# Norm and pooling work in half rows, placed by lateness, and down products added two banks at a time, in a streaming encoder step on one Trainium2 core

## The chip, the cores and the metric

The kernel runs on one core of one Trainium2 chip. The metric is device time in microseconds of one execution, on that core. The engines are TensorE (PE in the profile), VectorE (DVE), ScalarE (ACT), GpSimd (POOL) and SyncE (SP, which here only issues DMAs).

## The reference

Two layers over 1056 tokens (1024 of a prompt and 32 of a running stream), width 1024, float32. Cut to what matters:

```python
for i in range(2):
    y = short_conv_mixer(x) if i == 0 else pool_mixer(x)      # pooling: trailing means over 2, 4, 8, 16 frames, by four groups of channels
    h = layer_norm(ALPHA * x + y, ln1_g[i], ln1_b[i])          # called ("mix", i, group) below
    r = relu(h @ mlp_w1[i])                                    # 1024 -> 4096, the "up" products
    f = (r * r) @ mlp_w2[i]                                    # 4096 -> 1024, the "down" products
    e = (p[i] @ ple_w[i]) * sigmoid(h @ ple_gate_w[i])         # the "ple" and "gate" products
    x = layer_norm(ALPHA * h + f + e, ln2_g[i], ln2_b[i])      # called ("mlp", i, group)
```

In the pooling mixer, `d = means - x` and `y = (d @ w_grp) * scale`, with one 256x256 matrix for each of the four channel groups (the "grp" products).

## The kernel before, in words

Activations lie transposed: 128 features on the partitions, tokens along the free axis. The 1056 tokens are three groups (n = 0, 1, 2) of TG = 352, and a row of 1024 features is 8 blocks (KD) of 128 features. `acc` holds the residual of all three groups, 8x352 columns each. Every product is made in three matmuls on split operands (`triple`: high by high, high by low, low by high), so each weight and each activation has a high part, cast by ScalarE, and a low part, subtracted by VectorE. A weight unit of 128x1024 is loaded by SP into one of four raw buffers, cast (L727) and subtracted (L549); this is called a refill here.

The program is one list of steps, `plan`, and each engine walks through the whole list in order and does its part of each step. The kinds that matter:

- an up step: 24 matmuls on TensorE into one bank; then ScalarE makes relu (L841), square (L843) and the high part `r_hi` (L847); then VectorE subtracts the low part `r_lo` (L1042). Up steps come in pairs; they are called the first and the last up step here.
- a down step: 24 matmuls, 6 for each of four blocks, into four PSUM banks in turn; VectorE adds each bank to `acc` (L1046) and so frees it. Down steps come in pairs as well: the first for blocks 0 to 3, the second for blocks 4 to 7, in the same four banks. So the second cannot begin before VectorE has added block 0 of the first: the line is `pe.wait_ge(b_free, step.b + (i - 3))`.
- a gate step (24 matmuls) and a ple step (6 matmuls) for the gated embedding.

The usual order is up, up, down, down. The down steps use `r` of the pair of up steps before the last one, so TensorE doesn't wait for fresh `r` values.

After its own work of a step, an engine does first the step's refills and then the step's `side` list: the pieces of layer norm and pooling that the planner has hung on that step. VectorE and ScalarE do them in this order, and nothing of the next step overtakes them. The pieces of a norm on VectorE are sum (L935 to L937), mean (L966, subtracts the mean), vsum (the same tree on the squares), var (L971), rstd (L975 reciprocal, L977 to L979), norm (L983, multiplies) and lo (L986, the low part of the result); on ScalarE square, affine (L786) and hi (L803). TensorE makes the means with matmuls by ones, at L654 and L658. The pieces of pooling, for each of four windows, are fill (ScalarE copies to a window buffer), the running sums on GpSimd (L1126), centre (VectorE, L999, L1005, L1009), grp (12 matmuls on TensorE for two output blocks, which wait for centre's result) and gadd (VectorE, L1018).

Where each piece is hung is decided by `beside`: it goes through rows of (gap, cost, pieces), moves on by gap steps, and on until three steps in a row have `cost` microseconds left of what `room` gives them. LEAD says how many chunks of the MLP group 0 does alone, and how many groups 0 and 1 do together, before group 2 joins, in each layer.

Of the kernel before, what the change touches and what calls it, by code (L numbers as in the profile page):

```python
# [12 lines left out]
P = 128  # L13
# [23 lines left out]
LEAD = (5, 3), (9, 5)  # L37
# [6 lines left out]
MM_US, ADD_US, GATE_US, R_LO_US, SPLIT_US = 0.159, 0.52, 0.57, 0.61, 1.23  # L44
# [107 lines left out]
def make_plan():  # L152
# [99 lines left out]
    def room(step):  # L252

        own = len(step.refill) * SPLIT_US
        if step.kind == "down":
            return 24 * MM_US - own - 4 * ADD_US
        if step.kind == "up":
            return 24 * MM_US - own - R_LO_US
        if step.kind == "gate":
            return 30 * MM_US - own - 2 * GATE_US  # L260
        return 24 * MM_US - own - 2 * ADD_US

    def norm(i, done):

        n = NORMS.index(i)
        rows = [(0, 3.2, [("sum", n, done)]), (2, 3.1, [("mean", n)]), (1, 0, [("square", n)]), (1, 3.2, [("vsum", n)]), (2, 0.6, [("var", n)]),
                (1, 4.0, [("rstd", n)]), (1, 3.1, [("norm", n)]), (1, 0, [("affine", n, 0)]), (1, 0, [("affine", n, 1)])]
        if i[0] == "mix":
            rows += [(1, 0, [("hi", n)]), (1, 3.1, [("lo", n)])]
        return rows  # L270

    def pooling(n):
        rows = [(1, 0, [("fill", 4 * n)]), (1, 0, [("fill", 4 * n + 1)])]
        for q in range(len(WINDOWS)):
            rows.append((1, 3.0, [("centre", 4 * n + q)]))
            if q + 2 < len(WINDOWS):
                rows.append((0, 0, [("fill", 4 * n + q + 2)]))
            if q:
                rows.append((1, 1.1, [("grp", 8 * n + 2 * q - 2 + j, 4 + (q - 1) // 2) for j in range(2)]
                             + [("gadd", 8 * n + 2 * q - 2 + j) for j in range(2)]))  # L280
        rows.append((2, 1.1, [("grp", 8 * n + 6 + j, 5) for j in range(2)] + [("gadd", 8 * n + 6 + j) for j in range(2)]))
        return rows

    def beside(first, *chains, grp_from=0):


        steps = [s for s in plan[first:] if s.kind not in ("ple", "refill")]
        at = 0
        for row in (row for chain in chains for row in chain):
            gap, cost, parts = row  # L290
            at += gap
            while parts[0][0] == "grp" and plan.index(steps[at]) <= grp_from:
                at += 1
            while cost and sum(left[id(s)] for s in steps[at:at + 3]) < cost:
                at += 1
            steps[at].side += parts
            for s in steps[at:at + 3]:
                spent = min(cost, max(left[id(s)], 0))
                left[id(s)] -= spent
                cost -= spent  # L300
        return plan.index(steps[at])
# [37 lines left out]
    left = {}  # L339
# [4 lines left out]
    for step in plan:  # L344
        left[id(step)] = room(step)

# [36 lines left out]
def bass_streaming_trunk(nc, x_t, w_stream, p_t, vectors, conv_hist, pool_hist, y_t, conv_new, pool_new):  # L383
# [6 lines left out]
    with ExitStack() as ctx:  # L390
# [167 lines left out]
        def _(sp):  # L558
# [38 lines left out]
            for n in range(NG - 1):  # L597
                for h in range(2):

                    sp.wait_ge(affine, (len(NORMS) - NG + n) * 2 + h + 1)  # L600
# [11 lines left out]
        def _(pe):  # L612
# [25 lines left out]
            def side(what, i, *rest):  # L638
# [16 lines left out]
                elif what == "var":  # L655
                    pe.wait_ge(var_sum, i + 1)
                    pe.wait_ge(centred, i + 1)
# [16 lines left out]
            def do(step):  # L674
# [6 lines left out]
                elif step.kind == "gate":  # L681
                    if step.m == 0:
                        pe.wait_ge(h_ready, step.layer * NG + step.n + 1)
# [34 lines left out]
        def _(act):  # L718
# [43 lines left out]
            def side(what, i, *rest):  # L762
                if what == "finish":
# [4 lines left out]
                    side("var", i)  # L768
# [4 lines left out]
                elif what == "square":  # L773
                    act.wait_ge(centred, i + 1)
                    act.activation(grp(squares, NORMS[i][2]), grp(acc, NORMS[i][2]), ACT.Square).then_inc(squared, 1)
                elif what == "var":
# [4 lines left out]
                elif what == "affine":  # L781
                    kind, layer, n, at = norm_of(i)
                    h, = rest
                    act.wait_ge(normed, i + 1)
                    for k in range(4 * h, 4 * h + 4):
                        last = act.activation(blk(acc, n, k), blk(acc, n, k), ACT.Identity, bias=vcol(at + KD + k), scale=vcol(at + k))  # L786
                    last.then_inc(affine, 1)
                    if (kind, layer, h) == ("mlp", 0, 1):
                        act.wait_ge(affine, 2 * i + 2)
# [7 lines left out]
                elif what == "hi":  # L797
                    kind, layer, n, _ = norm_of(i)
                    act.wait_ge(affine, 2 * i + 2)
# [3 lines left out]
                    act.copy(grp(hh, n), grp(acc, n)).then_inc(ln_hi, 1)  # L803
                elif what == "fill":
# [3 lines left out]
                    act.wait_ge(affine, 2 * NORMS.index(("mlp", 0, n)) + 2)  # L808
# [64 lines left out]
        def _(dve):  # L873
# [59 lines left out]
            def tree(src, tmp, out, done):  # L933
                h = GCOLS // 2
                then(dve.tensor_tensor(tmp[:, 0:h], src[:, 0:h], src[:, h:2 * h], ALU.add))  # L935
                then(dve.tensor_tensor(tmp[:, 0:h // 2], tmp[:, 0:h // 2], tmp[:, h // 2:h], ALU.add))
                dve.tensor_tensor(out, tmp[:, 0:TG], tmp[:, TG:2 * TG], ALU.add).then_inc(done, 1)  # L937

            def over_blocks(ap):
                return ap.rearrange("p (a t) -> p a t", a=1).to_broadcast([P, KD, TG])  # L940

            def side(what, i, *rest):
                n = NORMS[i][2] if i < len(NORMS) else None
                if what == "finish":
# [4 lines left out]
                    side("rstd", i)  # L949
# [3 lines left out]
                elif what == "sum":  # L953
                    name, value = rest[0]
                    dve.wait_ge(sems[name], value)

                    wait(dve, mean_full, i)
                    tree(grp(acc, n), grp(squares, n), s_mean[:], mean_sum)
                elif what == "vsum":
                    dve.wait_ge(squared, i + 1)  # L960

                    wait(dve, rstd_done, i)
# [243 lines left out]
```

## Time and profile before

| | us |
|---|---|
| median of 3 runs | 2201.65 (2198.06 to 2203.07) |
| the profiled execution, its own time | 2200.9 |
| its span from first to last instruction | 2199.1 |
| TensorE matmuls busy | 2130.7 (97% of the span) |
| VectorE busy | 1255.0 (57%) |
| ScalarE busy | 807.3 (37%) |
| GpSimd busy | 70.3 (3%) |
| mean granted TensorE clock | 0.990 |

The share of a busy engine counts the time in which at least one of its instructions runs. Matmuls overlap (each record lasts about 0.32 us, and one begins every 0.16 us), so the time in which TensorE has no record is a little less than what a wait costs. The span leaves 1.8 us of the execution's own time outside.

### The profile page before, as it was taken

The numbers are of one execution on the slowest core, as the hardware profiler recorded it, in microseconds if no ns is written. First come the engines' busy times: TensorE is split into PE (matmuls) and PEld (weight loads), VectorE is DVE, ScalarE is ACT, GpSimd is POOL, SyncE is SP. The second block draws the span as 40 slices with busy tenths as digits, with TensorE's granted clock in tenths as the row PEclk, the third lists the DMA queues.
The fourth block names the chain that finished last, engine by engine and source line by source line (L and its number), as shares of the span: only waits on it lengthen the run. The fifth ranks groups of instructions, "written<-read, shape, count | busy, mean of one in ns | idle before, by whom it ended". The sixth has DMA issues, their size and how long they took to land. (4 is left out here: it accounts for less than half of the span.)

```text
span 2199.1 us, 31589 instructions
## 1 busy us (share of the span) xinstructions
PE 2130.7 (97%) x13166; PEld 2113.8 (96%) x13166; DVE 1255.0 (57%) x1823; ACT 807.3 (37%) x1233; POOL 70.3 (3%) x61
## 2 busy tenths in 40 slices
PE   8999999999999999999999999998989999999996
PEld 8999999999999999999999999998989999999996
DVE  4233367786454444445676777876755355444576
ACT  3122123654333222323444455455333224233343
POOL 0000000000000000000110030002000000000000
PEclk9999999999999999999999999999999999999998
DMA  4011141343132111111212434442213112122232
GB/s 168 29 57 39 56 134 65 113 134 125 55 106 77 39 57 40 46 51 39 68 68 70 129 115 150 136 134 70 77 55 96 58 49 66 53 75 77 77 116 99
DMA packets 51455, 179.67 MB, mean 82 GB/s; under 512 B 7936, under 2 KB 8064, under 8 KB 51328
## 3 DMA queue, kind: packets, MB, share of 16 engines
q1 hardware_dynamic: 49248, 177.72, 24.4%
q8 instruction: 95, 1.56, 0.3%
q10 hardware_dynamic: 2080, 0.12, 0.1%
q14 instruction: 32, 0.26, 0.0%
HBM read 173.36 MB, written 4.46 MB: 81 GB/s over the span
## 5 line engine op out<-in xcount | busy, mean ns | idle before, releaser
L616 PE MATMUL ps<-h_hi,w_split 128*128 128x352 f32 x2160 | 700.0, 324 | 4.8 <-DVE h_lo L921 2.1
L618 PE MATMUL ps<-h_hi,w_split 128*128 128x352 f32 x2160 | 692.8, 321 | 0.0
L617 PE MATMUL ps<-h_lo,w_split 128*128 128x352 f32 x2160 | 692.2, 320 | 0.0
L616 PE MATMUL ps<-r_hi,w_split 128*128 128x352 f32 x1632 | 536.5, 329 | 37.5 <-DVE acc L1046 37.5
L618 PE MATMUL ps<-r_hi,w_split 128*128 128x352 f32 x1632 | 528.3, 324 | 0.0
L617 PE MATMUL ps<-r_lo,w_split 128*128 128x352 f32 x1632 | 527.8, 323 | 0.0
L1046 DVE TENSOR_TENSOR acc<-acc,ps 128x352 f32<-128x352 f32 x768 | 376.4, 519 | 145.1 <-PE ps L618 143.9
L549 DVE TENSOR_TENSOR w_split<-w_raw,w_split 128x1024 fp32r<-128x1024 f32 x294 | 357.0, 1232 | 136.4 <-ACT w_split L727 135.7
L727 ACT CAST w_split<-w_raw 128x1024 fp32r<-128x1024 f32 x294 | 301.6, 1046 | 322.1 <-PE ps L618 316.5
L616 PEld LDWEIGHTS ps<-h_hi,w_split 128*128 128x128 f32 x2160 | 405.0, 187 | 7.6 <-issue 3.7
L617 PEld LDWEIGHTS ps<-h_lo,w_split 128*128 128x128 f32 x2160 | 406.4, 188 | 1.1
L618 PEld LDWEIGHTS ps<-h_hi,w_split 128*128 128x128 f32 x2160 | 404.9, 187 | 0.0
L616 PEld LDWEIGHTS ps<-r_hi,w_split 128*128 128x128 f32 x1632 | 310.0, 190 | 45.1 <-issue 34.5
L1042 DVE TENSOR_TENSOR r_lo<-t,r_hi 128x352 fp32r<-128x352 f32 x192 | 101.8, 530 | 434.3 <-ACT r_hi L847 434.3
L617 PEld LDWEIGHTS ps<-r_lo,w_split 128*128 128x128 f32 x1632 | 311.2, 191 | 1.2
L618 PEld LDWEIGHTS ps<-r_hi,w_split 128*128 128x128 f32 x1632 | 309.8, 190 | 0.0
L841 ACT ACTIVATE t<-ps 128x352 f32<-128x352 f32 x192 | 89.1, 464 | 570.5 <-PE ps L618 562.4
L616 PE MATMUL ps<-x_hi,w_split 128*128 128x352 f32 x576 | 186.4, 324 | 9.2 <-DVE w_split L549 9.2
L618 PE MATMUL ps<-x_hi,w_split 128*128 128x352 f32 x576 | 186.6, 324 | 0.0
L617 PE MATMUL ps<-x_lo,w_split 128*128 128x352 f32 x576 | 185.9, 323 | 0.0
L616 PEld LDWEIGHTS ps<-x_hi,w_split 128*128 128x128 f32 x576 | 108.7, 189 | 9.2 <-issue 9.2
L618 PEld LDWEIGHTS ps<-x_hi,w_split 128*128 128x128 f32 x576 | 109.9, 191 | 0.0
(80 smaller groups left out, 1118.2 us busy)
## 6 DMA issues: line engine op xcount, KB each, us to landing
w_raw<-w_stream SPq DMA_DIRECT2D x318, 512.0 KB, 3.5
x_raw<-x_t SPq DMA_DIRECT2D x6, 704.0 KB, 8.4
y_t<-acc SPq DMA_DIRECT2D x4, 704.0 KB, 4.1
w_raw<-p_t SPq DMA_DIRECT2D x6, 352.0 KB, 2.9
y_t<-acc SPq DMA_DIRECT2D x4, 352.0 KB, 2.4
pool_new<-acc ACTq DMA_DIRECT2D x2, 60.0 KB, 7.2
vec<-vectors SPq DMA_DIRECT2D x1, 78.0 KB, 7.2
pool_history<-pool_hist SPq DMA_DIRECT2D x1, 60.0 KB, 6.7
```

The source lines that it names most:

```text
L549: ins = eng.tensor_tensor(ws[:, slot, 1, :], raw[:, u.q, :], f32(ws[:, slot, 0, :]), ALU.subtract)
L616: pe.matmul(out, wh, mov_h, start=first, stop=False)
L617: pe.matmul(out, wh, mov_l, start=False, stop=False)
L618: return pe.matmul(out, wl, mov_h, start=False, stop=last)
L727: act.copy(ws[:, slot, 0, :], raw[:, u.q, :]).then_inc(w_hi, 1)
L841: act.activation(t, ps[:, step.bank, 0:TG], ACT.Relu).then_inc(a_free, 1)
L1042: dve.tensor_tensor(rpart(rl, *r), tt[:, step.bank, :], f32(rpart(rh, *r)), ALU.subtract).then_inc(r_ready, 1)
L1046: dve.tensor_tensor(blk(acc, step.n, m), blk(acc, step.n, m), ps[:, B_BANK + (step.bank + i) % 4, 0:TG], ALU.add).then_inc(b_free, 1)
```

## The change

Norm and centre pieces are cut: sum, centre (which "mean" did before), square, vsum, rstd, norm, hi and lo have two parts each, and affine four. Most of these are two instructions of 128x1408 where one of 128x2816 stood; sum, vsum and rstd have the same instructions in two parts. The piece of pooling on VectorE is called `centre_window` and has two parts, the second of which is the subtraction of L1009. The planner's rows carry a cost on VectorE and one on ScalarE, and the rule that places them is new: a piece goes on the first step at which neither engine would then be more than LATE_US behind. The rows of the grp products of group 0 come one after the other with their windows, those of groups 1 and 2 after all four windows. GpSimd's part is as before. In layer 1 group 0 does 8 chunks alone where it did 9. VectorE adds two PSUM banks at a time in all down steps but the last two.

```diff
-LEAD = (5, 3), (9, 5)
+LEAD = (5, 3), (8, 5)
-MM_US, ADD_US, GATE_US, R_LO_US, SPLIT_US = 0.159, 0.52, 0.57, 0.61, 1.23
+MM_US = 0.159
+DVE_US = {"split": 1.23, "down": 2 * 0.89, "up": 0.61, "gate": 2 * 0.57, "out": 2 * 0.53}
+ACT_US = {"split": 1.05, "down": 0, "up": 1.45, "gate": 0.5, "out": 0}
+LATE_US = 2.4
...
+    def own(step, table):
+        return table.get(step.kind, 0) + len(step.refill) * table["split"]
...
-        rows = [(0, 3.2, [("sum", n, done)]), (2, 3.1, [("mean", n)]), (1, 0, [("square", n)]), (1, 3.2, [("vsum", n)]), (2, 0.6, [("var", n)]),
-                (1, 4.0, [("rstd", n)]), (1, 3.1, [("norm", n)]), (1, 0, [("affine", n, 0)]), (1, 0, [("affine", n, 1)])]
+        rows = [(0, 1.7, 0, [("sum", n, 0, done)]), (0, 1.5, 0, [("sum", n, 1, done)]),
+                (2, 1.6, 0, [("mean", n), ("centre", n, 0)]), (0, 1.6, 0, [("centre", n, 1)]),
+                (1, 0, 1.3, [("square", n, 0)]), (0, 0, 1.3, [("square", n, 1)]),
+                (1, 1.7, 0, [("vsum", n, 0)]), (0, 1.5, 0, [("vsum", n, 1)]), (2, 0.6, 0, [("var", n)]), (1, 0, 0.5, [("root", n)]),
+                (1, 2.4, 0, [("rstd", n, 0)]), (0, 1.6, 0, [("rstd", n, 1)]),
+                (0, 1.6, 0, [("norm", n, 0)]), (0, 1.6, 0, [("norm", n, 1)])]
+        rows += [(q == 0, 0, 1.35, [("affine", n, q)]) for q in range(4)]
...
+            rows += [(1, 1.6, 0, [("centre_window", 4 * n + q, 0)]), (0, 1.0, 0, [("centre_window", 4 * n + q, 1)])]
+            products.append((1, 1.1, 0.6 * 2, [("grp", 8 * n + 2 * q + j, 4 + q // 2) for j in range(2)]
+                             + [("gadd", 8 * n + 2 * q + j) for j in range(2)]))
+            if n == 0:
+                rows.append(products.pop())
...
+        def late(table, which, cost):
+            total = 0
+            for i, step in enumerate(steps[:at + 1]):
+                took = (30 if step.kind == "gate" else 24) * MM_US
+                total = max(0, total - took) + own(step, table) + taken[which].get(id(step), 0)
+            return max(0, total + cost - took)
...
-            while cost and sum(left[id(s)] for s in steps[at:at + 3]) < cost:
+            while ((parts[0][0] == "grp" and plan.index(steps[at]) <= grp_from)
+                   or (dve_us and late(DVE_US, "dve", dve_us) > LATE_US) or (act_us and late(ACT_US, "act", act_us) > LATE_US)):
                 at += 1
...
+                elif step.kind == "down" and not step.final:
+                    for i in range(0, len(step.blocks), 2):
+                        k, bank = step.blocks[i], B_BANK + (step.bank + i) % 4
+                        dve.wait_ge(b_full, step.b + (i + 2))
+                        two = grp3(acc, step.n)[:, k:k + 2, :]
+                        dve.tensor_tensor(two, two, ps[:, bank:bank + 2, 0:TG], ALU.add).then_inc(b_free, 2)
```

The first place in VectorE's order is the norm ("mix", 1, 1), in layer 0's last chunks. Before, from the down step that carries its var to the next up steps:

```order
L1042 TENSOR_TENSOR r_lo<-t,r_hi 128x352
L971 TENSOR_SCALAR var<-ps 128x352
L1046 TENSOR_TENSOR acc<-acc,ps 128x352 x4
L549 TENSOR_TENSOR w_split<-w_raw,w_split 128x1024
L1046 TENSOR_TENSOR acc<-acc,ps 128x352 x4
L549 TENSOR_TENSOR w_split<-w_raw,w_split 128x1024 x2
L975 RECIPROCAL std<-std 128x352
L977 SCALAR_TENSOR_TENSOR rstd<-std 128x352
L978 TENSOR_TENSOR rstd<-rstd,var 128x352
L979 SCALAR_TENSOR_TENSOR rstd<-rstd,std 128x352
L1042 TENSOR_TENSOR r_lo<-t,r_hi 128x352
```

And of the change, around the same reciprocal (L998), where L1071 is the `r_lo` of the last up step and L1077 the adds of the first down step:

```order
L553 TENSOR_TENSOR w_split<-w_raw,w_split 128x1024
L1071 TENSOR_TENSOR r_lo<-t,r_hi 128x352
L998 RECIPROCAL std<-std 128x352
L1001 SCALAR_TENSOR_TENSOR rstd<-std 128x352
L1002 TENSOR_TENSOR rstd<-rstd,var 128x352
L1003 SCALAR_TENSOR_TENSOR rstd<-rstd,std 128x352
L1008 TENSOR_TENSOR acc<-acc,rstd 128x1408
L1077 TENSOR_TENSOR acc<-acc,ps 128x704 x2
```

The reciprocal and its three followers stood behind the second down step; now they and half of the multiplication stand between the last up step's `r_lo` and the first down step's adds.

The second place is VectorE in the pooling of group 0. Before, the piece of window 0 and what stands around it:

```order
L1042 TENSOR_TENSOR r_lo<-t,r_hi 128x352 x2
L1046 TENSOR_TENSOR acc<-acc,ps 128x352 x8
L549 TENSOR_TENSOR w_split<-w_raw,w_split 128x1024 x2
L996 TENSOR_TENSOR win_54<-win_54,vec 128x2x15
L999 SCALAR_TENSOR_TENSOR win_54<-win_54,acc 128x2x352
L1005 CAST h_hi<-win_54 128x704
L1009 TENSOR_TENSOR h_lo<-win_54,h_hi 128x704
L1042 TENSOR_TENSOR r_lo<-t,r_hi 128x352
```

And of the change:

```order
L1071 TENSOR_TENSOR r_lo<-t,r_hi 128x352 x2
L1030 TENSOR_TENSOR win_54<-win_54,vec 128x2x15
L1033 SCALAR_TENSOR_TENSOR win_54<-win_54,acc 128x2x352
L1039 CAST h_hi<-win_54 128x704
L1018 TENSOR_TENSOR h_lo<-win_54,h_hi 128x704
L1077 TENSOR_TENSOR acc<-acc,ps 128x704 x2
L1047 SCALAR_TENSOR_TENSOR acc<-acc,y_scaled_t 128x352 x2
```

The window stood behind two down steps and their refills, and its products came three steps later; now it stands behind the last up step's `r_lo`, and the grp products that need it (their gadd is L1047) come behind TensorE's very next step.

The third place is the start of the norm ("mix", 1, 1), where the ple weights are loaded. Before, the refills of four units (L549 x4) and the whole sum stood behind a second down step:

```order
L549 TENSOR_TENSOR w_split<-w_raw,w_split 128x1024 x4
L935 TENSOR_TENSOR ln_squares<-acc 128x1408
L936 TENSOR_TENSOR ln_squares<-ln_squares 128x704
L937 TENSOR_TENSOR sum_mean<-ln_squares 128x352
L1042 TENSOR_TENSOR r_lo<-t,r_hi 128x352
```

And of the change:

```order
L1071 TENSOR_TENSOR r_lo<-t,r_hi 128x352
L553 TENSOR_TENSOR w_split<-w_raw,w_split 128x1024 x2
L943 TENSOR_TENSOR ln_squares<-acc 128x1408
L1077 TENSOR_TENSOR acc<-acc,ps 128x704 x2
L553 TENSOR_TENSOR w_split<-w_raw,w_split 128x1024
```

Two of the refills and the first part of the sum now stand between a last up step's `r_lo` and the first down step's adds.

## Rows read from the trace of the kernel before

**Rows 1.** The page: its head and the busy time of PE and DVE.

```profile
span 2199.1 us, 31589 instructions
PE 2130.7 (97%) x13166; PEld 2113.8 (96%) x13166; DVE 1255.0 (57%) x1823; ACT 807.3 (37%) x1233; POOL 70.3 (3%) x61
```

**Rows 2.** Waits of PE, whole span: us in total, times, longest.

```profile
PE ps L616 <- DVE acc L1046: 37.5, 19, 5.5
...
PE ps L616 <- DVE acc L1025: 2.1, 2, 1.5
```

**Rows 3.** The same by stretch: 270:520, 1000:1200, 1500:1650, 1650:2150.

```profile
PE ps L616 <- DVE acc L1046: 2.0, 2, 1.7
...
PE ps L616 <- DVE acc L1046: 10.4, 6, 2.5
...
PE ps L616 <- DVE acc L1046: 20.4, 6, 5.5
...
PE ps L616 <- DVE acc L1046: 3.1, 2, 1.9
```

**Rows 4.** Timeline of DVE at one wait: start us, us, instruction, [idle before].

```profile
1184.78 0.53 DVE L1042 TENSOR_TENSOR r_lo<-t,r_hi 128x352 fp32r<-128x352 f32 x1 [3.33 <-ACT r_hi L847]
1185.22 3.08 DVE L986 TENSOR_TENSOR h_lo<-acc,h_hi 128x2816 fp32r<-128x2816 f32 x1
1188.22 2.42 DVE L1046 TENSOR_TENSOR acc<-acc,ps 128x352 f32<-128x352 f32 x5
```

**Rows 5.** Timeline of PE there: a pair of down steps begins, stops, restarts.

```profile
1183.02 0.32 PE L616 MATMUL ps<-r_hi,w_split 128*128 128x352 f32 x1
...
1186.70 0.32 PE L618 MATMUL ps<-r_hi,w_split 128*128 128x352 f32 x1
1188.88 0.40 PE L616 MATMUL ps<-r_hi,w_split 128*128 128x352 f32 x1 [1.86 <-DVE acc L1046]
```

**Rows 6.** Timeline of DVE where two refills follow a last up step.

```profile
1577.32 0.53 DVE L1042 TENSOR_TENSOR r_lo<-t,r_hi 128x352 fp32r<-128x352 f32 x1 [1.10 <-ACT r_hi L847]
1578.27 2.36 DVE L549 TENSOR_TENSOR w_split<-w_raw,w_split 128x1024 fp32r<-128x1024 f32 x2 [0.43 <-ACT w_split L727]
1580.55 2.41 DVE L1046 TENSOR_TENSOR acc<-acc,ps 128x352 f32<-128x352 f32 x5
```

**Rows 7.** Groups of DVE: busy us, mean ns of one, idle before.

```profile
L966 DVE TENSOR_TENSOR acc<-acc,ps 128x2816 f32<-128x2816 f32 x11 | 33.9, 3081 | 0.0
...
L975 DVE RECIPROCAL std<-std 128x352 f32<-128x352 f32 x12 | 28.2, 2347 | 0.6 <-ACT std L780 0.6
...
L936 DVE TENSOR_TENSOR ln_squares<-ln_squares 128x704 f32<-128x704 f32 x22 | 19.6, 892 | 0.8
...
L935 DVE TENSOR_TENSOR ln_squares<-acc 128x1408 f32<-128x1408 f32 x11 | 17.8, 1622 | 0.2
...
L977 DVE SCALAR_TENSOR_TENSOR rstd<-std 128x352 f32<-128x352 f32 x12 | 6.3, 525 | 0.4
```

**Rows 8.** Timeline of DVE: one piece of a window, GpSimd idle, and adds behind it.

```profile
1096.71 0.89 DVE L999 SCALAR_TENSOR_TENSOR win<-win,acc 128x704 f32<-128x704 f32 x1
...
1098.20 0.89 DVE L1009 TENSOR_TENSOR h_lo<-win,h_hi 128x704 fp32r<-128x704 f32 x1
1099.01 1.81 DVE L1046 TENSOR_TENSOR acc<-acc,ps 128x352 f32<-128x352 f32 x4
```

**Rows 9.** Timeline of DVE: window and gadd while GpSimd runs.

```profile
1529.33 3.46 DVE L999 SCALAR_TENSOR_TENSOR win<-win,acc 128x640 f32<-128x640 f32 x2
...
1537.57 3.37 DVE L1018 SCALAR_TENSOR_TENSOR acc<-acc,y_scaled_t 128x352 f32<-128x352 f32 x2
```

**Rows 10.** Windows: busy us of PE, PEld, DVE, ACT, POOL, then PEclk, DMA.

```profile
1190.00:1195.00 5.00, 5.00 (x23) 5.00 (x22) 2.02 (x5) 0.09 (x1) 0.00 (x0) 0.66 0.01 3
```

**Rows 11.** Timeline of ACT ahead of the longest wait.

```profile
1510.67 2.39 ACT L786 ACTIVATE acc<-acc,vec 128x352 f32<-128x352 f32 x4
...
1515.60 0.48 ACT L847 CAST r_hi<-t 128x352 fp32r<-128x352 f32 x1
```

More of the change, by code:

```diff
@@ new lines, in pooling @@
+            if n == 0:
+                rows.append(products.pop())
+            if q + 2 < len(WINDOWS):
+                rows += [(n > 0, 0, 1.0, [("fill", 4 * n + q + 2)])]
+        return rows + products
+    def beside(first, *chains, grp_from=0):
+        steps = [s for s in plan if s.kind not in ("ple", "refill")]
+        at = next(i for i, s in enumerate(steps) if plan.index(s) >= first)
+        def late(table, which, cost):
[4 more added lines that the diff above has]
+            return max(0, total + cost - took)
+        for gap, dve_us, act_us, parts in (row for chain in chains for row in chain):
@@ L291, in beside @@
             at += gap
-            while parts[0][0] == "grp" and plan.index(steps[at]) <= grp_from:
-                at += 1
-            while cost and sum(left[id(s)] for s in steps[at:at + 3]) < cost:
+            while ((parts[0][0] == "grp" and plan.index(steps[at]) <= grp_from)
+                   or (dve_us and late(DVE_US, "dve", dve_us) > LATE_US) or (act_us and late(ACT_US, "act", act_us) > LATE_US)):
                 at += 1
             steps[at].side += parts
[L297 to L300, printed above, removed]
+            for which, cost in (("dve", dve_us), ("act", act_us)):
+                taken[which][id(steps[at])] = taken[which].get(id(steps[at]), 0) + cost
@@ L682, in do @@
                     if step.m == 0:
-                        pe.wait_ge(h_ready, step.layer * NG + step.n + 1)
+                        pe.wait_ge(h_ready, 2 * (step.layer * NG + step.n + 1))
                     if step.a < 2:
@@ L773, in side @@
                 elif what == "square":
-                    act.wait_ge(centred, i + 1)
-                    act.activation(grp(squares, NORMS[i][2]), grp(acc, NORMS[i][2]), ACT.Square).then_inc(squared, 1)
-                elif what == "var":
+                    n, h = NORMS[i][2], rest[0]
+                    act.wait_ge(centred, 2 * i + h + 1)
+                    act.activation(half(squares, n, h), half(acc, n, h), ACT.Square).then_inc(squared, 1)
+                elif what == "root":
                     act.wait_ge(var_copied, i + 1)
@@ L798, in side @@
                     kind, layer, n, _ = norm_of(i)
-                    act.wait_ge(affine, 2 * i + 2)
+                    h, = rest
+                    act.wait_ge(affine, 4 * i + 2 * h + 2)
                     if layer == 0:
                         act.wait_ge(out_full, (8, 20, 24)[n])
-                    act.copy(grp(hh, n), grp(acc, n)).then_inc(ln_hi, 1)
+                    act.copy(half(hh, n, h), half(acc, n, h)).then_inc(ln_hi, 1)
                 elif what == "fill":
@@ L972, in side @@
                 elif what == "rstd":
-                    dve.wait_ge(std_done, i + 1)
-                    wait(dve, normed, i)
-                    then(dve.reciprocal(std[:], std[:]))
+                    part, = rest
+                    if part == 0:
+                        dve.wait_ge(std_done, i + 1)
+                        wait(dve, normed, 2 * i)
+                        steps[0] += 1
+                        dve.reciprocal(std[:], std[:]).then_inc(ln_step, 1)
+                        return
+                    dve.wait_ge(ln_step, steps[0])
                     then(dve.scalar_tensor_tensor(out=rstd[:], in0=std[:], scalar=-0.5, in1=std[:], op0=ALU.mult, op1=ALU.mult))
```

112 lines of the change are left out of this document (54 added, 58 removed).

## The prediction

> **What bounds the kernel now.** I read the page first: TensorE has a matmul in flight for 97% of the span, VectorE is busy for 57%, ScalarE for 37% [rows 1]. So the number of matmuls sets the time (the change adds and takes away none), and what can move is the time in which TensorE stands still. Next the waits of TensorE over the span: 37.5 us in 19 waits go to VectorE's adds of down products, and 2.1 to those of the out products [rows 2]. By stretch they lie where norms and pooling run beside the MLP: 10.4 us around 1100, 20.4 around 1575, 3.1 in layer 1, 2.0 in the head [rows 3]; all other waits for the adds are worth 1.6. Last the timeline of one wait, on both engines, for its anatomy.
>
> **The rule of one wait.** A first down step begins on TensorE at 1183.02 [rows 5]. The last up step's `r_lo` starts 1.76 us later, at 1184.78, and the next instruction of VectorE at 1185.22, so 2.20 us after the up step's end; before that the engine was idle, waiting for ScalarE [rows 4]. There stands lo, 3.00 us from its start to that of the first add at 1188.22 [rows 4]. TensorE restarts at 1188.88, 0.66 us after that start; its last matmul began at 1186.70, so it was due at 1186.86, 3.84 us after it began [rows 5]. With S the work on VectorE between the last up step's `r_lo` and the first add, the loss is 2.20 + S + 0.66 - 3.84 = S - 0.98, here 2.02 (the profile calls 1.86 of it idle). Work behind the first down step's adds, behind the second down step or on the first up step costs nothing: VectorE is idle for 3.3 us ahead of this `r_lo` [rows 4], and that idle time is the cover. The place of a piece decides, not its length alone.
>
> **The add over two banks.** No row has one. A lower bound is the 704-column subtraction, whose successor starts 0.81 us later (1098.20 to 1099.01), against 0.43 us a piece for single adds (four in 1.81, the last lasting 0.52) [rows 8]. An upper bound is two singles without overlap, 1.04. I take 0.81, same shape and engine. VectorE saves 2 x 0.43 - 0.81 = 0.05 us a pair, so nothing that counts, and TensorE gets block 0 back 0.38 us later: the loss becomes S - 0.60. With S = 0 the slack of 0.60 hides it, at the upper bound too (0.37 left), so the 480 us in which no norm runs stay as they are. If the add is at its upper bound, the thirty or so waits below grow by 0.23 us each, 7 us in all.
>
> The Trainium skill speaks for this edit (VectorE: DVE Perf Modes, the section on the errata with its cycle table): a PSUM-source instruction costs 120 cycles beside its columns at 0.96 GHz, and one should minimise their number. By that, an estimate, a down step's adds fall from 1.97 to 1.72 us, 48 us over 190 steps. Here the singles start 0.43 us apart, under the page's 0.49 [rows 8], and the saved time lies on an engine that mostly idles.
>
> **Halves.** A whole row of 2816 columns lasts 3.08 and one of 1408 lasts 1.62 [rows 7]; from start to start I take 1.53 for a half (0.43 plus 1056 columns of the 2.57 us for 2464 that separate the two shapes). Two halves are 3.06 where 3.00 stood: nothing, unless they are placed apart.
>
> **Where the pieces now stand.** The order of the change on each engine, against the rule, gives every S. The single losses of before that I set against them are read as in [rows 5], one restart for each wait, and add up to the totals of [rows 2, 3]. Pieces that were behind a down step or on a first up step, and now stand at a last up step, are new losses.
>
> - Second part of rstd (three followers of 0.53 each, 1.6) and the first half of norm (1.53), the reciprocal being on the first up step and about 0.15 late: S = 3.3, loss 2.7, in five norms (groups 0 and 1 after each MLP, and the mixer norm of group 0): 13.3. Before, three of the five had a whole norm there at about 2.0, 6.1 in all.
> - Both halves of the mean's subtraction: S = 3.06, less 0.6 since the mean matmuls hold up the down step by as much: 1.9, in four norms: 7.4. Before two, 1.4 each: 2.9.
> - The whole sum or vsum of three instructions (1.62 + 0.89 + 0.53, S = 3.0 [rows 7]): 2.4 for the third mixer norm of layer 0 and 2.4 for the vsum of ("mix", 1, 1); lo of ("mix", 1, 0) 2.5, was 2.0. The head had 1.9 for the whole rstd of that third norm. Sum 7.3 against 3.9.
> - The first place of the order above: reciprocal 2.35, three followers and half a norm, S = 5.5, loss 4.9, in the mixer norms of groups 1 and 2: 9.8. Against it stand three waits of before in group 2's norm (vsum, norm, lo), 3.0, 2.6 and 3.3 with what they lost beside their idle time: 8.9.
> - The third place: with two refills there the adds begin 3.23 us after `r_lo` (1577.32 to 1580.55 [rows 6]), so 4.99 after the up step; then 1.6 of the sum: 4.99 + 1.6 + 1.04 - 3.84 = 3.8. Before, the same refills of group 2 cost 1.8.
> - Group 0's pooling, the second place: a window is 2.3 us [rows 8] with 0.2 for the ratio, so its result comes at 2.2 + 2.5 = 4.7 or later, and the grp matmuls want it 3.84 after the up step. While GpSimd adds, VectorE's two-input instructions take twice to three times as long (3.46 for the two parts of one window's first step, 3.37 for two gadds of 0.53 each [rows 9]). I take 1.5, 1.0, 2.0 and 1.0 for the four windows and 1.5 for the sum behind the last: 7.0; before 2.7.
> - Group 2's pooling: ScalarE has three quarters of affine (four instructions take 2.39 [rows 11]), the rest and two DMA issues ahead of the fills. ScalarE's queue from the end of the first up step behind the gates: 2.6 until VectorE's gated adds let relu begin, 1.45 for relu to cast, affine 3.45, 1.45, affine 1.15, DMA issues 1.5, 1.45, a refill 0.95, two fills 2.0, 1.45, which makes 17.45; the last up step ends at 11.9. So its `r_hi` is 5.6 us behind it instead of 1.7. In [rows 11] ScalarE's `r_hi` comes behind four affines in the same way, ahead of the wait of 5.5 [rows 3]. The window behind it is 3 to 5: loss 5.6 + 0.5 + 4 + 1.04 - 3.84 = 7.3, then 3.7 for a later window, and 0.4. Together 11.4; before 10.6, of which one idle time is the 5.5.
> - ScalarE late by affine and hi elsewhere, and single halves: lo and sum of group 1, 3.4; vsum's second part 1.4; hi of group 2, 0.95; half a subtraction 1.0. Sum 6.7; before 1.3.
> - Two refills between down steps that follow each other, and the like: 2.9, was 3.2. Waits in the out products: 0.7, was 2.4; the norm of 3 us there is now in halves.
> - LEAD: four refills of 318 fewer, hidden. The next gates find their h ready 15 us or more ahead, by the order.
>
> Sum after 70.3, before 43.8 (37.5 and 2.1 of idle time, and 0.17 lost beside it in each of some 24 waits, is 43.7): **26.5 us more**.
>
> **The clock.** After 1188.88 the granted clock is 0.66 on average over 1190 to 1195, so at half, 1.2 GHz, for 3.4 us of them, in which a matmul starts every 0.293 us: 23 matmuls where 31 fit [rows 10], 1.2 to 1.5 us lost. Before there are seven such stretches, after all four waits over 3 us and three of the eight between 1.8 and 2.8. After the change I count six losses above 3 and thirteen in the middle class: six and about six, five or six more, **8 us**.
>
> 2200.9 + 26.5 + 8 = 2235.4 for the profiled execution, which lies 0.75 below the median of its kernel: **2236**. From 18 + 3 (no contention with GpSimd at the windows, ScalarE less late, few clock falls) to 45 + 15 (pair at its upper bound, everything a little later) it is 2222 to 2262; I widen the lower end for places that I may have misread.
>
> **The rivals.**
>
> - *Faster: halves let the adds through.* What makes TensorE wait is a long instruction in front of an add; with half the length and the lateness bound of 2.4, losses shrink below the slack. Speaks for it: 20.4 us lie in one stretch [rows 3], where pieces of 3.00 stand. Against it: both halves often stand in the same slot, and the planner counts a last up step's 3.84 us as room, where VectorE can begin only 2.20 after them. It decides from the point at which S stays under 0.6 in most slots. If all losses to adds went, 41 us and 10 of clock: 2150; if half, 2175. The skill's rule on instruction count, if VectorE's load were what TensorE waits for, leads to 2153 by its own figures; from rows, 0.05 x 380 pairs = 19 us gives 2182.
> - *Nothing: new waits pay for the old.* The 20.4 shrink by ten and the early norms grow by ten: 2200. For it speaks that long losses cost clock as well; against it the five-fold 2.7.
> - *Slower by the pairs alone.* If an add over two banks took over 1.41 (2.20 + 1.41 + 0.23 = 3.84), all 95 pairs of down steps would wait; each 0.1 us above is 9.5 us. At 1.6 that is 18, and 0.8 in each of some thirty losses 24: 2278, beyond the range. Nothing of 704 columns is that slow without GpSimd [rows 7, 8].
>
> **Chances.** The forecast (2210 to 2262) 0.79, more than that 0.05; faster 0.11, nothing 0.05. What a measurement of this kernel can tell from no change is 0.2%, 4.4 us. So faster 0.11, same 0.05, slower 0.84. The range 2208 to 2262 leaves out faster, nothing and the far end, together 0.2.
>
> **What would show it.** TensorE's waits for the adds (now L1077) near 60 us in 30 or more; one of about 4.7 after each of two reciprocals that follow a last `r_lo`; five of about 2.5; waits of grp matmuls for `h_lo` of 1 to 2 in group 0's pooling; no wait between 520 and 1000; pairs starting 0.8 apart; a mean clock of 0.98. Wrong would be the forecast if VectorE starts the pieces of a last up step earlier than 2.2 us after it, or if the order on the chip's engines let adds pass them.

## The result and the profile after

The changed kernel takes 2264.6 us (median of four, 2255.58 to 2265.44) against 2201.35 for the kernel before on the same chip (2198.06 to 2203.07): a ratio of 1.028 (95% interval 1.0251 to 1.0309). It is slower, as forecast, but by 63 us and not 35: the time is 2.6 us beyond the upper end of the forecast's range (2208 to 2262).

The page of the profiled execution (its own time 2263.78), to be held against [rows 1]:

```profile
span 2262.0 us, 31620 instructions
PE 2152.9 (95%) x13166; PEld 2133.5 (94%) x13166; DVE 1219.3 (54%) x1467; ACT 805.5 (36%) x1246; POOL 67.2 (3%) x61
```

TensorE has the same 13166 matmuls; VectorE has 356 instructions less and 35.7 us less to do. So less work, and a longer span. The waits of TensorE over the span (against [rows 2]):

```profile
PE ps L620 <- DVE acc L1077: 63.5, 26, 7.3
...
PE ps L620 <- ACT t L847: 5.3, 5, 2.0
PE ps L620 <- issue: 5.0, 3, 3.3
PE ps L620 <- ACT t L841: 3.7, 2, 3.1
...
PE ps L620 <- DVE acc L1054: 1.7, 1, 1.7
```

37.5 us of waits for the adds have become 63.5, in 26 and not 19, the longest 7.3 and not 5.5. Beside them stand 14 us of a sort that hardly existed before: for ScalarE's relu (L847) and sigmoid (L841), and "issue", three waits of grp matmuls; each of them restarts 0.1 us after the end of the subtraction L1018 that finishes the window it needs, so the window had come late. By stretch, 270:520, 1000:1220, 1220:1530, 1530:1700 and 1700:2200 (against [rows 3]; the later stretches are shifted by what has been lost):

```profile
PE ps L620 <- DVE acc L1077: 4.5, 3, 2.3
...
PE ps L620 <- DVE acc L1077: 12.1, 6, 2.9
...
PE ps L620 <- DVE h_lo L1018: 2.1, 1, 2.1
...
PE ps L620 <- DVE acc L1077: 19.1, 7, 5.2
PE ps L620 <- ACT t L841: 3.7, 2, 3.1
PE ps L620 <- ACT t L847: 2.0, 1, 2.0
...
PE ps L620 <- DVE acc L1077: 18.2, 5, 7.3
...
PE ps L620 <- DVE acc L1077: 9.2, 4, 2.9
```

Nothing waits between 520 and 1000. The stretch 1220 to 1530 is now the dearest; before, all that [rows 3] doesn't name came to 1.6. Its longest wait, on VectorE and then on TensorE (columns as in [rows 4, 5]):

```profile
1433.22 0.53 DVE L1071 TENSOR_TENSOR r_lo<-t,r_hi 128x352 fp32r<-128x352 f32 x1 [1.98 <-ACT r_hi L853]
1433.66 2.35 DVE L998 RECIPROCAL std<-std 128x352 f32<-128x352 f32 x1
1436.04 0.53 DVE L1001 SCALAR_TENSOR_TENSOR rstd<-std 128x352 f32<-128x352 f32 x1
...
1437.72 1.62 DVE L1008 TENSOR_TENSOR acc<-acc,rstd 128x1408 f32<-128x1408 f32 x1
1439.26 1.68 DVE L1077 TENSOR_TENSOR acc<-acc,ps 128x704 f32<-128x704 f32 x2
```

```profile
1434.78 0.32 PE L622 MATMUL ps<-r_hi,w_split 128*128 128x352 f32 x1
1440.29 0.63 PE L620 MATMUL ps<-r_hi,w_split 128*128 128x352 f32 x1 [5.19 <-DVE acc L1077]
1440.72 0.49 PE L621 MATMUL ps<-r_lo,w_split 128*128 128x352 f32 x1
```

S is 1439.26 - 1433.66 = 5.60 (foreseen 5.5), the loss 1440.29 - 1434.78 - 0.16 = 5.35 (4.9). TensorE restarts 1.03 after the adds' start, for a pair of which two take 1.68, so one has a pitch of 0.80. The matmul behind the restart lasts 0.49 and not 0.32: the granted clock is at half, 1.2 GHz, which the window over 1441 to 1448 shows as 0.74 on average (against [rows 10]):

```profile
1441.00:1448.00 7.00, 7.00 (x35) 7.00 (x35) 3.33 (x4) 1.57 (x2) 0.00 (x0) 0.74 0.24 77
```

The adds as a group (singles: [rows 4, 8]) and the half of norm ([rows 7]):

```profile
L1077 DVE TENSOR_TENSOR acc<-acc,ps 128x704 f32<-128x704 f32 x380 | 333.5, 885 | 226.7 <-PE ps L622 225.6 <-issue 0.5
...
L1008 DVE TENSOR_TENSOR acc<-acc,rstd 128x1408 f32<-128x1408 f32 x22 | 35.5, 1621 | 0.3
```

**The sum.** Taken as the prediction takes it (each gap between two matmuls' starts, less 0.159), the span grew by 62.9 us: 43.9 in gaps over 0.47 us, 12.2 in matmuls at half clock (91 more of them), 1.7 in small gaps, and 5.4 that are spread over all the others; 0.3 less at the end. The last term is no finding: single runs of one kernel differ by as much.

### The profile page after: what moved, and what is told of

It is laid out like the page before. It is cut to its first block, busy times and chain, and to the rows that moved or that the text cites. A ratio compares the mean times of both kernels' runs of the same rounds, so it can differ in the third digit from the quotient of the medians.

```text
span 2262.0 us, 31620 instructions
## 1 busy us (share of the span) xinstructions
PE 2152.9 (95%) x13166; PEld 2133.5 (94%) x13166; DVE 1219.3 (54%) x1467; ACT 805.5 (36%) x1246; POOL 67.2 (3%) x61
## 4 chain that ended last, share of the span: by engine, by line
PE 83%; DVE 8%; ACT 6%; issue 3%; DMA 0%; ACTq 0%; DVEq 0%
PE ps L620 28%; PE ps L622 27%; PE ps L621 27%; ACT w_split L731 2%; ACT acc L791 1%; DVE acc L1077 1%; DVE std L998 1%; DVE w_split L553 1%; ACT t L849 1%; ACT t L847 1%; DVE win L1033 1%; DVE r_lo L1071 0%; DVE ln_squares L943 0%; ACT r_hi L853 0%; DVE acc L1066 0%
## 5 line engine op out<-in xcount | busy, mean ns | idle before, releaser
L620 PE MATMUL ps<-r_hi,w_split 128*128 128x352 f32 x1632 | 543.6, 333 | 63.5 <-DVE acc L1077 63.5
L622 PE MATMUL ps<-r_hi,w_split 128*128 128x352 f32 x1632 | 534.6, 328 | 0.0
L621 PE MATMUL ps<-r_lo,w_split 128*128 128x352 f32 x1632 | 533.8, 327 | 0.0
L1077 DVE TENSOR_TENSOR acc<-acc,ps 128x704 f32<-128x704 f32 x380 | 333.5, 885 | 226.7 <-PE ps L622 225.6
L553 DVE TENSOR_TENSOR w_split<-w_raw,w_split 128x1024 fp32r<-128x1024 f32 x290 | 355.3, 1242 | 131.4 <-ACT w_split L731 131.0
L620 PEld LDWEIGHTS ps<-r_hi,w_split 128*128 128x128 f32 x1632 | 315.0, 193 | 72.3 <-issue 69.0
L1071 DVE TENSOR_TENSOR r_lo<-t,r_hi 128x352 fp32r<-128x352 f32 x192 | 102.1, 532 | 450.3 <-ACT r_hi L853 450.1
L621 PEld LDWEIGHTS ps<-r_lo,w_split 128*128 128x128 f32 x1632 | 316.6, 194 | 1.5
L622 PEld LDWEIGHTS ps<-r_hi,w_split 128*128 128x128 f32 x1632 | 314.6, 193 | 0.0
L847 ACT ACTIVATE t<-ps 128x352 f32<-128x352 f32 x192 | 88.9, 463 | 600.3 <-PE ps L622 587.1
L620 PEld LDWEIGHTS ps<-x_hi,w_split 128*128 128x128 f32 x576 | 108.8, 189 | 9.2 <-issue 9.2
L621 PEld LDWEIGHTS ps<-x_lo,w_split 128*128 128x128 f32 x576 | 110.2, 191 | 0.0
```

The source lines that it names most:

```text
L553: ins = eng.tensor_tensor(ws[:, slot, 1, :], raw[:, u.q, :], f32(ws[:, slot, 0, :]), ALU.subtract)
L620: pe.matmul(out, wh, mov_h, start=first, stop=False)
L621: pe.matmul(out, wh, mov_l, start=False, stop=False)
L622: return pe.matmul(out, wl, mov_h, start=False, stop=last)
L847: act.activation(t, ps[:, step.bank, 0:TG], ACT.Relu).then_inc(a_free, 1)
L1071: dve.tensor_tensor(rpart(rl, *r), tt[:, step.bank, :], f32(rpart(rh, *r)), ALU.subtract).then_inc(r_ready, 1)
```

## A wait that the prediction didn't have

All four windows of group 1 now stand on gate steps, one on every other of them; in the kernel before two of the four did. ScalarE shows four sigmoids there:

```profile
1312.03 0.46 ACT L841 ACTIVATE t<-ps 128x352 f32<-128x352 f32 x1 [5.70 <-DVE acc L1066]
...
1316.42 0.46 ACT L841 ACTIVATE t<-ps 128x352 f32<-128x352 f32 x1 [2.20 <-DVE acc L1066]
1316.79 1.04 ACT L731 CAST w_split<-w_raw 128x1024 fp32r<-128x1024 f32 x1
1323.51 0.46 ACT L841 ACTIVATE t<-ps 128x352 f32<-128x352 f32 x1 [5.68 <-DVE acc L1066]
...
1327.90 0.46 ACT L841 ACTIVATE t<-ps 128x352 f32<-128x352 f32 x1 [2.20 <-DVE acc L1066]
```

And VectorE and TensorE between the second and the third of them:

```profile
1317.86 2.27 DVE L553 TENSOR_TENSOR w_split<-w_raw,w_split 128x1024 fp32r<-128x1024 f32 x1 [1.52 <-ACT w_split L731]
1320.06 0.88 DVE L1033 SCALAR_TENSOR_TENSOR win<-win,acc 128x704 f32<-128x704 f32 x1
1320.97 0.53 DVE L1039 CAST h_hi<-win 128x704 fp32r<-128x704 f32 x1
1321.53 0.89 DVE L1018 TENSOR_TENSOR h_lo<-win,h_hi 128x704 fp32r<-128x704 f32 x1
1322.34 0.51 DVE L1064 TENSOR_TENSOR t<-t,ps 128x352 f32<-128x352 f32 x1
1322.89 0.53 DVE L1066 SCALAR_TENSOR_TENSOR acc<-acc,t 128x352 f32<-128x352 f32 x1
```

```profile
1324.12 0.40 PE L620 MATMUL ps<-h_hi,w_split 128*128 128x352 f32 x1 [0.57 <-ACT t L841]
...
1337.10 0.40 PE L620 MATMUL ps<-h_hi,w_split 128*128 128x352 f32 x1 [3.09 <-ACT t L841]
...
1343.13 0.40 PE L620 MATMUL ps<-h_hi,w_split 128*128 128x352 f32 x1 [1.98 <-ACT t L847]
```

This is a circle through two in-order queues. The sigmoid waits for a gated add (L1066); the cast of the refill stands behind the sigmoid, VectorE's subtraction waits for the cast, the window stands behind the subtraction, the next gated add behind the window, and the next sigmoid waits for that. From sigmoid to sigmoid it is 4.39 us without a window (1312.03 to 1316.42, its L1066 lasting 1.18 beside GpSimd and not 0.53, so 3.74 without that) and 7.09 with one; a gate step with its ple step, 30 matmuls, takes TensorE 4.77. A piece of over 1 us (4.77 - 3.74) makes its own round longer than the step, and VectorE's idle time (1.52 ahead of the subtraction) is no room, since it lies inside the circle. A round without a piece wins back 0.4 to 1.0 us, so two rounds with one window last 4.39 + 7.09 = 11.48 where TensorE's two steps last 9.54, and the lateness grows from window to window. TensorE then waits for a bank that ScalarE hasn't read: it loses 0.73 at 1324.12, 3.25 at 1337.10 and, waiting for a relu, 2.14 at 1343.13. How much of this GpSimd adds by slowing VectorE no run separates.

A piece on a gate step is thus not a loss by itself. In the kernel before, two windows and whole norm pieces stood on gate steps too:

```profile
1294.75 0.89 DVE L999 SCALAR_TENSOR_TENSOR win<-win,acc 128x704 f32<-128x704 f32 x1
...
1300.79 2.09 DVE L999 SCALAR_TENSOR_TENSOR win<-win,acc 128x704 f32<-128x704 f32 x1
1302.91 1.59 DVE L1005 CAST h_hi<-win 128x704 fp32r<-128x704 f32 x1
```

The two windows follow four rounds without a piece, and TensorE waited for a sigmoid once, 0.26 us by the profile, at 1311.52. By these rows long pieces cost when too few free rounds lie around them; experiment 6 tests it.

## The experiments

All ratios are to the kernel before on the same chip, with 95% intervals; medians of three or more runs each. "Rule" means that no piece of more than 0.6 us on VectorE stands on a last up step (experiment 4), "both rules" that in addition the last gate steps and, for windows, all gate steps are kept free (experiment 7).

| kernel | us | ratio |
|---|---|---|
| change | 2264.6 | 1.028 (1.0251 to 1.0309) |
| its planner with LEAD (10, 5) | 2255.27 | 1.0242 (1.022 to 1.0263) |
| change, single adds | 2242.32 | 1.0186 (1.0161 to 1.021) |
| before, pairs alone | 2213.85 | 1.0062 (1.004 to 1.0084) |
| before, halves, group 1's norm and windows where the change has them | 2211.53 | 1.005 (1.0033 to 1.0067) |
| before, halves in place | 2198.72 | 0.9992 (0.9978 to 1.0005) |
| change, rule, LEAD (10, 5) | 2177.96 | 0.9898 (0.9878 to 0.9917) |
| change, both rules, LEAD (11, 5) | 2167.62 | 0.9853 (0.9835 to 0.9872) |
| before with the rule | 2165.66 | 0.9854 (0.983 to 0.9877) |
| before with the rule, halves | 2164.12 | 0.9833 (0.9807 to 0.9859) |
| change, both rules, LEAD (11, 5), single adds | 2160.97 | 0.9818 (0.9799 to 0.9837) |

**1. The change with single adds.** The branch of the pairs is taken out:

```diff
-                elif step.kind == "down" and not step.final:
-                    for i in range(0, len(step.blocks), 2):
-                        ...
-                        dve.tensor_tensor(two, two, ps[:, bank:bank + 2, 0:TG], ALU.add).then_inc(b_free, 2)
```

> The change with VectorE's adds of down products one bank at a time again; every piece stays where the change puts it. Theory of place (a loss is S - 0.60 with pairs and S - 0.98 with single adds, S being VectorE's work between the last up step's r_lo and the first add): each of the 26 waits for the adds shrinks by 0.38 us, 10 us in all, and one or two falls of the clock go, so 2250 to 2254, with the waits of 2 to 7 us still there. Rival, the pairs are the cost (two banks held longer, or a slow two-bank read): back to 2200 to 2215. Rival, halving itself is the cost: no change, 2264.

Measured: 2242.32, below the 2250 to 2254, and at neither rival's value. The waits for the adds are 0.26 to 0.45 shorter, most of them by 0.36 or 0.37 (1.87 to 1.50, 3.09 to 2.73, 2.49 to 2.08, 5.35 to 4.99), the total 9.6 less:

```profile
PE ps L620 <- DVE acc L1075: 53.9, 24, 6.9
```

The gaps in all give 13.4 us, of which 1.6 is the wait for the relu behind the gates (2.14 to 0.57) and 1.8 lies in the last norm's matmuls by ones, and the clock 3.4; the medians lie 22 apart, and the rest, some 5 us, is spread over all the other matmuls and unexplained. With single adds the change is still 1.9% slower, so most of the loss is the order.

**2. The pairs alone,** the same branch in the kernel before.

> The kernel before with the two-bank adds alone. Theory of place: its 19 waits for the adds grow by 0.38 us each, 7 us, perhaps one more fall of the clock: 2207 to 2211, and no wait between 520 and 1000 us. Rival, the pairs are the cost: 2240 or more. A pair starts 0.81 us after the one before it.

Measured: 2213.85, above the 2207 to 2211. Most waits go up by 0.34 to 0.45 (1.44 to 1.81, 2.04 to 2.40), one by 1.14 (4.95 to 6.09), and six that the slack had hidden appear, of 0.39 to 0.59 each:

```profile
PE ps L616 <- DVE acc L1048: 46.6, 25, 5.9
```

None lies between 520 and 1000. In the profiled execution the waits cost 9.9 us more (53.7 for 43.9), and 38 more matmuls run at half clock, 5.3 us, where the expectation had one more fall. A pair returns block 0's bank when both banks are added, and only that bank is waited for.

**3. The halves alone.** Before's planner and places, with each piece expanded into its parts where it stands:

```diff
+        if what in ("sum", "square", "vsum", "rstd", "norm", "hi", "lo"):
+            return [(what, i, h) + rest for h in range(2)]
```

> The kernel before with every piece cut as the change cuts it, both parts standing where the whole piece stood (the planner and LEAD of before), single adds. Theory of place: two halves last 0.06 us longer than the whole, so 2201 to 2204. Rival, halving is the cost (more instructions, more semaphores between the engines): 2215 or more. Rival of the forecast's faster case, halves let adds through: 2190 or less.

Measured: 2198.72, under the 2201 to 2204 but not to be told from the kernel before (ratio 0.9978 to 1.0005). Cutting costs nothing and brings nothing.

**4. The change without VectorE's pieces at a last up step,** with LEAD (10, 5), since this rule makes the pooling's end later:

```diff
-LEAD = (5, 3), (8, 5)
+LEAD = (5, 3), (10, 5)
...
+                   or (dve_us > 0.6 and steps[at].kind == "up" and steps[at + 1].kind == "down")
```

> The change with one more condition in the planner: no piece of more than 0.6 us on VectorE stands on an up step that is followed by a down step. The later norms need more room by it, so group 0 of layer 1 does 10 chunks alone instead of 8. Theory of place: of TensorE's 63.5 us of waits for the adds all but some 15 go, and most falls of the clock: 2195 to 2215, if the pieces now crowded into the gate steps cause no new waits. Rivals (pairs or halving are the cost): above 2245.

Measured: 2177.96, better than the 2195 to 2215, 87 us under the change and 1% under before; waits for the adds fall from 63.5 to

```profile
PE ps L621 <- DVE acc L1078: 17.5, 10, 4.7
```

**5. The control for LEAD:** the change with (10, 5) alone.

> The change with 10 chunks alone in layer 1 and nothing else different, a control for the run with the last-up rule (2178). All theories: the order of steps changes little and LEAD costs nothing by itself, 2258 to 2266.

Measured: 2255.27, under the 2258 to 2266. By the medians LEAD is worth 9 us and the rule the other 77, but LEAD isn't neutral: it moves pieces. Waits for the adds are 55.9 us here and not 63.5, those for the sigmoid 9.4 and not 3.7. The rule in turn takes away waits for ScalarE as well, from 11.5 us in all here to 4.0 in experiment 4, so the 77 aren't the last up steps' alone.

**6. The gate steps alone.** Experiment 3's kernel, in which group 1's norm and windows are hung by a table on the steps that they have in the change (gates and what leads to them), and all else as before.

```diff
+             269: [("centre_window", 4, 0), ("centre_window", 4, 1)], 271: [("fill", 6)],
+             273: [("centre_window", 5, 0), ("centre_window", 5, 1)], 275: [("fill", 7)],
...
+        step.side = [x[:3] + (done,) if x[0] == "sum" else x for x in moved.get(at, [])] + step.side
```

> The halves in place (the plan of before, 2198.7 us) with one stretch of the plan as the change has it: the norm behind layer 0's MLP of group 1, and all four windows of its pooling on gate steps; single adds. Theory of the chain between the engines (on a gate step VectorE's piece stands between the refill's subtraction and the gated add, ScalarE's next sigmoid waits for that add, its cast for the sigmoid, VectorE's subtraction for the cast, so a gate step lasts 3.8 us plus the piece, and more than 1 us of piece makes the next ones late): waits of TensorE for ScalarE around the end of the gate steps of 0.8 to 1.0, 3.2 to 3.4 and 0.6 us, where the kernel before has one of 0.3; with the two last-up places of the norm (1.5 and 2.7) and a fall of the clock 2207 to 2211. Rival, the slack of 7 us that the prediction gave the gate steps: only the 1.5 and 2.7, 2202 to 2204.

Measured: 2211.53, at the upper end of the 2207 to 2211 and 12.8 above experiment 3. (The "slack of 7 us" that this expectation ascribes to the prediction stands nowhere in it; the prediction has no term for group 1's gate steps.) Two waits for the sigmoid, 0.97 and 3.38, appear:

```profile
PE ps L643 <- ACT t L864: 4.0, 2, 3.2
```

The norm's two places at last up steps appear as well, 1.50 and 2.73, so about half of the new waits is the gates' (4.35 against 4.23). The third wait at the gates, for relu behind them, stays away; with single adds in the change it is 0.57, and why it is 2.14 in the change itself stays open. So four windows on gate steps make the circle's two waits for the sigmoid, without pairs and without the rest of the new order.

**7. Both rules, single adds.** No pair, nothing at a last up step, no window on a gate step, nothing over 0.6 us on the last three gates of a visit; LEAD (11, 5):

```diff
+                   or (dve_us > 0.6 and steps[at].kind == "gate" and (parts[0][0] == "centre_window" or steps[at].m > 4))
```

> The change with single adds, no VectorE piece over 0.6 us on an up step that is followed by a down step, no window on a gate step and no such piece on the last three gate steps; 11 chunks alone in layer 1, which that needs. Theory of place and of the chain in the gate steps: against the first rule alone (2178) the 0.36 us of some ten waits for adds (3 to 4), the waits for ScalarE of 4 us and those behind them (7) go, and a fall or two of the clock: 2162 to 2172. Rival, what is left is not the planner's: 2175 to 2180.

Measured: 2160.97, just under the 2162 to 2172 and 1.8% under the kernel before: the lowest of all. It differs from experiment 4 in three things, the adds, the second rule and LEAD; experiment 10 takes the adds out. No run takes the second rule and LEAD (11, 5) apart.

```profile
PE ps L622 <- DVE acc L1077: 11.2, 7, 3.4
```

In its longest wait, 3.55 us at 1567.98, VectorE's piece is a window beside GpSimd:

```profile
1561.59 3.75 DVE L1035 SCALAR_TENSOR_TENSOR win<-win,acc 128x640 f32<-128x640 f32 x2
```

**8. The last-up rule in the kernel before,** nothing else:

```diff
-            while cost and sum(left[id(s)] for s in steps[at:at + 3]) < cost:
+            while cost and (sum(left[id(s)] for s in steps[at:at + 3]) < cost
+                            or (cost > 0.6 and steps[at].kind == "up" and steps[at + 1].kind == "down")):
```

> The kernel before, whole pieces and single adds, its own planner and LEAD, with the one condition that no piece over 0.6 us on VectorE stands on an up step that is followed by a down step. Theory of place: TensorE's 37.5 us of waits for the adds fall by the seven that such pieces cause (some 17 us, with five falls of the clock 24): 2176 to 2188. Rival, halves are needed for the gain of the run with 2178: no better than 2195.

Measured: 2165.66, better than the 2176 to 2188: whole pieces and the old planner, one more condition, 1.5% faster. Waits for the adds go from 37.5 to

```profile
PE ps L617 <- DVE acc L1047: 12.5, 8, 5.5
```

**9. The same with halves in place.**

> The run with the planner of before and the last-up rule (2165.7 us), with every piece in two parts in its place. Theory of place: the places count and the cutting does not, 2162 to 2169. Rival, halves bring something once the places are right: 2155 or less.

Measured: 2164.12. Its interval overlaps those of experiments 8 and 7: with the rule, halves and lateness add little if anything.

**10. Experiment 7 with pairs.**

> The run with both rules (2161.0 us), with the two-bank adds again. Theory of place: the pairs cost 0.36 us in each wait for the adds that is left, seven waits, 2.5 us, and maybe a fall of the clock: 2162 to 2167. Rival, the pairs cost more than the waits show (between the change and its run with single adds the medians lie 22 us apart, the waits 13): 2170 or more.

Measured: 2167.62, at the upper end of the 2162 to 2167 and 6.7 above experiment 7; the waits say 4 to 5:

```profile
PE ps L622 <- DVE acc L1079: 15.3, 10, 3.6
```

Against experiment 4, which has pairs too, the second rule and LEAD (11, 5) bring 10 us together, and the waits for relu and sigmoid, 4.0 us by the profile, are gone.

## Why the prediction was right, and where it failed

The forecast was 2236 (2208 to 2262), the time 2264.6. In the profiled executions the growth is 62.9 for 34.5, and the 28.4 between them are 17.4 in the waits (43.9 for 26.5), 4.2 of clock (12.2 for 8) and 7.1 spread over other matmuls, less 0.3. The upper end was missed by 2.6 us only, less than any of the three, so the amounts below matter more than which side of it the time fell on.

- **Direction and main mechanism: right.** S - 0.98 for singles and S - 0.60 for pairs priced the losses at last up steps closely. Both halves of the mean's subtraction: 1.87 in four places (foreseen 1.9). Whole sum or vsum: 2.49 twice (2.4). Third place: 3.72 (3.8). Reciprocal behind a last `r_lo`: 5.35 and 5.00 (4.9). Longest: 7.45 (7.3). Mean clock: 0.982 (0.98). Experiments 4 and 8 show that this place is what costs most, in either planner.
- **"Second part of rstd and half of norm", 2.7 each: a size.** It is 3.09 four times and 3.04 once, 15.4 us in all for 13.3. With "the reciprocal about 0.15 late", `r_lo` was to start 1.91 after the up step; it started 2.32 after, held back by the reciprocal to 1067.40.
- **The add over two banks: right in size,** 0.80 for 0.81, and in the quiet 480 us. "Losses grow by 0.38" was 0.36. But "slack hides it" held only where nothing stands in S: experiment 2 shows six small new waits. Its 12 us are the 9.9 of its waits and some more falls of the clock.
- **The step that failed:** "Pieces that were behind a down step or on a first up step, and now stand at a last up step, are new losses", used as if there were no others. Pieces on gate steps had no term of loss (only group 2's item has relu's late start behind the gates); they were put at nothing, as they nearly were before. There TensorE lost 6.1 in group 1's visit and, with both halves of norm on the last but one gate step of the head and ScalarE's affine behind it, 1.25, 0.75 and 1.5 of 1.69 at the up steps after. That is 9.6 of the 17.5 us by which the gaps exceeded the 70.3 (87.8). The 1.03 and 0.92 in group 2's visit are of the same kind by the trace: the same halves of norm stand on the same gate step, and relu waits 3.52 for the gated add. For group 1's two waits for the sigmoid, 4.0 of the 6.1, experiment 6 shows the cause, and it makes 4.35 of them; for the head and group 2 it is read from the trace only (in the head relu waits 5.41 for the gated add). Experiments 7 and 10 agree: with the last gates kept free, TensorE has no wait for relu or sigmoid left that the profile lists.
- **The other sizes.** Group 0's windows and sum: 2.26, 0.99, 3.43, 1.08 and 1.61, together 9.4 for 7.0; the third of them was foreseen as 2.0. No run isolates the new order of these products. Group 2: 4.77 for 3.7 at the second window and, ahead of the longest wait, the 1.03 and 0.92 of the gates (the prediction's 0.95 is for ScalarE late by hi, and no hi stands there). Out products: 1.87 for 0.7. Against that the small single places and refills came to 8.3 for 10.1, so part of the error cancelled by luck.
- **The clock:** 12.2 for 8. There are twelve waits above 3 us in the body and not six, and ten of them are followed by a stretch at half clock, as are four between 2.49 and 2.9. Behind the two others, 1118.83 and 1337.10, the granted clock is 1.00 in the windows of 7 us that follow; why, stays open. Of the twelve, five are the 3.09 and 3.04 priced at 2.7, one is the 3.43 priced at 2.0, and one the 3.25 of the gates. So this is mostly not the gates' error again: 14 stretches came where about twelve were counted, and behind the waits of 3.72, 4.77 and 5.00 there are 16 or 17 matmuls at half clock, where before there were 9 to 12 behind each.
- **The rivals.** "Halves let the adds through" fails by experiment 3, and by the places: halves behind one another are a whole. "The pairs alone" fell by the pitch of 0.80. The Trainium skill says that one large tile pays the fixed latency once and many small ones pay it each (VectorE: DVE Perf Modes, the section on the errata), and so advises large tiles. Merged adds did lower VectorE's load, by 36.4 us in experiment 2 (1255.0 to 1218.6), where the prediction had an estimate of 48 by the Trainium skill's figures and 19 from rows. The runs speak against following the advice at this place: experiments 2 and 10 are slower than their partners with twice the adds.

Open are the 5.4 us spread over all matmuls, some 5 of the 22 us between the change and experiment 1, and the 2.14 behind group 1's gates.

## What to carry to other kernels

On an engine that mostly idles, the place of a piece decides: give each step kind the time from when the engine can begin to when the next release is due, not the length of the step. Where two in-order engines wait for each other round a circle, idle time inside the circle isn't room; take the circle's length from one release to the next and compare it with the step, and leave free rounds behind a long piece. Merge instructions only where nobody waits for the first half's result: one condition in the old planner, keeping long pieces off the slot ahead of the adds, brought 1.5%, and the merged adds cost 0.3 to 1% in each of three comparisons.

## What the runs showed of the hardware

How much VectorE slows while GpSimd runs depends on where its operands lie. In the lines above, the subtraction L553 (two operands in SBUF) takes 2.27 beside GpSimd's running sums, alone 1.22, and the window's first part 3.75 for two of 640 columns where 0.88 stood for 704 without it. A row of GpSimd at that time:

```profile
1314.30 4.75 POOL L1161 TENSOR_TENSOR win<-win 128x732 f32<-128x732 f32 x3 [6.73 <-ACT win L823]
```

And of VectorE, whose first line reads one operand from PSUM and whose second reads both from SBUF:

```profile
1314.61 0.52 DVE L1064 TENSOR_TENSOR t<-t,ps 128x352 f32<-128x352 f32 x1
1315.15 1.18 DVE L1066 SCALAR_TENSOR_TENSOR acc<-acc,t 128x352 f32<-128x352 f32 x1
```

L1064 kept its 0.52, L1066 took 1.18 where it takes 0.53 at 1322.89. Nor did any of the 768 single adds of the kernel before, which read PSUM, last over 0.523, though some ran beside GpSimd. The Trainium skill names the reason (GPSIMD Engine Reference, Specifications: GpSimd shares its SBUF interfaces with VectorE, in contention with instructions of two SBUF inputs); the trace agrees, and gives the size: a factor of 1.9 to 2.3 in these lines, and 3.2 for the gadds of [rows 9]. It isn't there in every case: in the kernel before, the subtraction L549 at 1299.64 took 1.23 while the profile has GpSimd running from 1298.19 to 1304.12 (its records are rough), and the cast L1005 at 1302.91, which reads one operand, took 1.59 where it takes 0.53 at 1295.67.
